# A hybrid decoder layer with expert rows: 32 columns move from the small token group to the large one

## The reference, cut to what matters

```
def _trunk(x, ...):
    xn = _rmsnorm(x, g_mix)
    xr, yr, ca, cb, ga, gb = _split_cols(xn @ w_in)
    ... branch_a = (h * gelu(yr)) @ w_a          # RG-LRU branch
    ... branch_b = silu(layernorm(dc)) @ w_b     # convolution branch
    merged = sigmoid(ga) * branch_a + sigmoid(gb) * branch_b
    x = x + merged @ w_out
    x = x + _peer(_rmsnorm(x, g_ffn), w_q, keys1, keys2, u_tab, v_tab)
    return _rmsnorm(x, g_final)

def block(xb):                                   # _peer, 8 heads, 16 experts per head
    q = (xb @ w_q).reshape(128, 8, 2, 128)
    s1 = einsum('thd,hkd->thk', q[:, :, 0], keys1); s2 = ... q[:, :, 1], keys2
    v1, i1 = top_k(s1, 16); v2, i2 = top_k(s2, 16)
    sv, si = top_k(v1[..., :, None] + v2[..., None, :], 16)
    e = i1[si // 16] * 128 + i2[si % 16]; g = softmax(sv)
    act = gelu(einsum('thkd,td->thk', u_tab[e], xb))
    return einsum('thk,thkd->td', g * act, v_tab[e])
```

## Time and profile before

| | us |
|---|---|
| median of 3 runs (lowest, highest) | 3867.29 (3864.64, 3870.36) |
| the profiled execution | 3870.63 |
| its span | 3868.8 |
| first product pair of the large group starts | 917.5 |
| last scores of the large group end | 1857.1 |
| first dot of the loop over r | 1912.4 |
| dot 256 of that loop starts | 2791.5 |

### The profile page before, as it was taken

The page is one execution under the profiler, slowest core; times in us unless marked ns, Lnnn a source line. Parts: engine busy times, 40 slices in busy tenths (PEclk is TensorE's granted clock), DMA queues, the critical chain, the costliest instruction groups (busy, mean ns, idle before and its releaser), DMA issues.

```text
span 3868.8 us, 34526 instructions
## 1 busy us (share of the span) xinstructions
PE 3051.7 (79%) x11870; PEld 1937.8 (50%) x11870; DVE 2591.0 (67%) x3611; ACT 586.0 (15%) x1115; POOL 1394.5 (36%) x876
## 2 busy tenths in 40 slices
PE   6999989987999989888345544544179899999993
PEld 6999989975555545555112212222143334444441
DVE  2788830035777766666688887889985556665658
ACT  4444320010010000111100001222250000000000
POOL 2000000003343333324476667666612234434344
PEclk9999999989999999999676677777599999999996
DMA  4222367759899998889899999999849999999998
GB/s 125 85 84 85 97 188 241 238 191 353 327 383 391 369 380 333 321 339 355 339 410 405 407 401 404 357 383 378 316 182 350 365 408 418 421 421 421 421 422 357
DMA packets 394596, 1244.91 MB, mean 322 GB/s; under 512 B 22785, under 2 KB 268289, under 8 KB 268959
## 3 DMA queue, kind: packets, MB, share of 16 engines
q0 software_dynamic: 120720, 876.60, 56.4%
q1 hardware_dynamic: 258944, 356.03, 26.4%
q10 hardware_dynamic: 14815, 10.87, 0.9%
HBM read 1232.26 MB, written 12.00 MB: 322 GB/s over the span
## 4 chain that ended last, share of the span: by engine, by line
DMA 35%; PE 27%; DVE 20%; issue 10%; POOL 5%; ACT 1%; SPq 1%; DVEq 0%; POOLq 0%; ACTq 0%
DMA region<-in_v_tab_dram,region 26%; PE ps L1588 14%; DVE region L1418 6%; DMA region<-in_u_tab_dram,region 5%; POOL region L607 5%; DVE region L1366 4%; PE ps L1571 3%; PE ps L1573 3%; PE ps L1572 3%; DVE region L1357 1%; DMA region<-in_w_q_dram 1%; DMA region<-scores_kept 1%; DVE region L1315 1%; DVE region L1312 1%; DMA region<-in_w_in_dram 1%
## 5 line engine op out<-in xcount | busy, mean ns | idle before, releaser
L607 POOL DMA_INDIRECT region<-in_u_tab_dram,region x544 | 886.8, 1630 | 1488.5 <-DVE region L1357 578.8
L1588 PE MATMUL ps<-region,region 128*128 128x160 f32 (+1 forms) x5120 | 1208.7, 399 | 67.3 <-DMA region<-in_w_out_dram 20.1
L1588 PEld LDWEIGHTS ps<-region,region 128*128 128x128 f32 x5120 | 852.2, 194 | 415.5 <-issue 43.1
L1418 DVE SCALAR_TENSOR_TENSOR region<-region,region 128x2048 f32<-128x2048 f32 x384 | 869.5, 2287 | 105.0 <-DMA region<-in_u_tab_dram,region 104.3
L1818 PE MATMUL ps<-region,region 128*128 128x512 f32 x2048 | 890.4, 597 | 38.8 <-DMA region<-in_v_tab_dram 38.0
L1366 DVE SCALAR_TENSOR_TENSOR region<-region,region,region 128x2048 f32<-128x2048 f32 x224 | 526.8, 2352 | 560.5 <-DMA region<-in_v_tab_dram,region 548.9
L1818 PEld LDWEIGHTS ps<-region,region 128*128 128x128 f32 x2048 | 389.7, 191 | 538.9 <-issue 483.2
L607 POOL DMA_INDIRECT region<-in_v_tab_dram,region x288 | 469.5, 1630 | 423.8 <-DVE region L1366 338.6
L1766 PE MATMUL ps<-region,region 128*128 128x512 f32 x512 | 355.8, 861 | 330.3 <-DMA region<-in_v_tab_dram,region 305.7
L1766 PEld LDWEIGHTS ps<-region,region 128*128 128x128 f32 x512 | 139.2, 285 | 532.2 <-issue 505.9
L1357 DVE SCALAR_TENSOR_TENSOR region<-region,region 128x2048 f32<-128x2048 f32 x160 | 363.0, 2286 | 17.7 <-DMA region<-in_u_tab_dram,region 17.6
(11 more groups left out here) (227 smaller groups left out, 1681.0 us busy)
## 6 DMA issues: line engine op xcount, KB each, us to landing
region<-in_v_tab_dram SPq DMA_DIRECT2D x128, 1024.0 KB
region<-in_w_in_dram SPq DMA_DIRECT2D x192, 512.0 KB
region<-in_w_out_dram SPq DMA_DIRECT2D x64, 512.0 KB
region<-in_w_q_dram SPq DMA_DIRECT2D x64, 512.0 KB
region<-in_w_a_dram SPq DMA_DIRECT2D x32, 512.0 KB
region<-in_w_b_dram SPq DMA_DIRECT2D x32, 512.0 KB
region<-in_u_tab_dram,region POOLq DMA_INDIRECT x544, 12.0
region<-in_x_prompt_dram SPq DMA_DIRECT2D x7, 1024.0 KB, 16.1
```

The lines of the kernel that those rows point to most:

```text
L607: pool.indirect_dma_start(out=slot, out_offset=None, in_=rows_ap, in_offset=bass.IndirectOffsetOnAxis(ap=idx[:, k:k + 1], axis=0)).then_in ...
L1418: stt(out=u_b[s], in0=u_b[s], scalar=1.0, in1=xn_tile(UNITS_A + u), op0=ALU.mult, op1=ALU.mult, accum_out=dots[u % 2][:, k:k + 1]).then_in ...
L1588: last = mm(outs[n][:, 0:WIDTH[g]], wide[s][:, q, n * P:(n + 1) * P], rhs(k), start=(k == 0), stop=(k == n_k - 1))
```

## The change

The small group becomes 128 columns: the last 96 prompt tokens and the 32 samples. The large group becomes `WB` = 416 columns: 384 and the 32 prompt tokens in front of those 96. These 32 prompt tokens are now the folded tile (units 8 and 9); its rows and scores come with the large group. The tile of units 0 to 7 holds 96 prompt tokens and the samples. `ROWS_W` is 128 instead of 96: DVE adds every value row of units 0 to 7, and PE's diagonal products keep the 32 of the folded tile (`ROWS_P` = 32, one every 7 dots). The count of gathers is the same.

```
-NA, NBT = P + TS, 3 * P
-COLS = (slice(NBT, T), slice(0, NBT))
-WIDTH = (NA, NBT)
-TILES = (slice(0, 2), slice(2, 5))
+NBT = 3 * P
+WB = NBT + TS
+PA = P - TS
+COLS = (slice(WB, T), slice(0, WB))
+WIDTH = (P, WB)
+TILES = (slice(0, 1), slice(1, 5))
...
-ROWS_W = 6 * TOPK
+ROWS_W = HEADS * TOPK
-VALUE_AT = {V_LAG + v * (ROWS_A - V_LAG) // ROWS_W: v for v in range(ROWS_W)}
+VALUE_AT = {V_LAG + v: v for v in range(ROWS_W)}
...
-STEPS_NORM = (118, 121)
+STEPS_1, STEPS_2, STEPS_3 = 14, 80, 96
+STEPS_NORM = (STEPS_3, STEPS_3 + 3)
...
-def steps_branch(m):
-    return 14 + 21 * m // 2, 14 + 21 * (m + 1) // 2
+def steps_branch(i):
+    return STEPS_1 + (STEPS_2 - STEPS_1) * i // PAIRS, STEPS_1 + (STEPS_2 - STEPS_1) * (i + 1) // PAIRS
...
-    return 98 + 2 * min(j, 10), 98 + 2 * min(j + 1, 10)
+    return STEPS_2 + (STEPS_3 - STEPS_2) * j // DC, STEPS_2 + (STEPS_3 - STEPS_2) * (j + 1) // DC
...
-    return 121 + 39 * h // HEADS, 121 + 39 * (h + 1) // HEADS
+    first = STEPS_NORM[1]
+    return first + (ROWS_W - first) * h // HEADS, first + (ROWS_W - first) * (h + 1) // HEADS
...
             for p in range(ROWS_A + 1):
+                if p == ROWS_W:
+                    for q in range(SLOTS_V + 1):
+                        small_value(p - 1 + q)
...
-                if p - 1 in VALUE_AT:
-                    v = VALUE_AT[p - 1]
-                    if v >= SLOTS_V:
-                        pool.wait_ge(v_added, v - SLOTS_V + 1)
-                    value_row(v)
+                if p != ROWS_W:
+                    small_value(p - 1 if p < ROWS_W else p - 1 + SLOTS_V)
...
             for h in range(2, HEADS):
-                fifth_tile(h)
                 expert_steps(*STEPS_Q[h])
...
             for h in range(HEADS):
                 expert_steps(*steps_query(h))
+                fifth_tile(h)
+            route(HEADS)
+            expert_steps(ROWS_W, ROWS_A)
...
                 pe.wait_ge(s_read[j], HEADS * g + h + 1)
-                pe.wait_ge(s4_read[j], (h if g == 0 else HEADS) + 1)
-                for t in range(2 + g):
+                pe.wait_ge(s4_read[j], h * g + 1)
+                for t in range(1 + 3 * g):
```

137 lines of the change are left out of this document (75 added, 62 removed).

## The result

The changed kernel takes 4028.05 us in the median of 4 runs (4024.89 to 4029.80), the kernel before 3865.97 (4 runs) on the same chip: a ratio of 1.0419, with a 95% interval of 1.0400 to 1.0437. It is slower by 162 us, where 118 was forecast. The profiled execution has a span of 4026.6 us against 3868.8.

The account below looks back on a forecast made before the run. PE was taken to bound both column groups, DVE and DMA the work up to dot 256. Small group -66, large group +73, gap +180 and loop -69 gave +118 on 3867.3, so 3985 us, range 3925 to 4035.

Parts of the forecast that it names:

- the forecast's own band: Whole kernel: a time of 3960 to 4010 us around the forecast of 3985, chance 0.45.
- rival (2): Large group: handshakes between DVE, ACT and PE slow heads and trips, giving 4010 to 4025 us; chance 0.16.
- Small group, -66: Small group: narrower passes, less norm work and fewer waits start the large group 66 us earlier, at about 851.
- Rival (3): Small group does not shrink, because of PE's weight loads or the full queue: +52 at most, 4037 us; chance 0.07.
- Gap, +180: Last scores to the loop's first dot: late expert steps make it 235 us instead of 55; bounds +135 and +215.
- Rival (1): Gap: gathers keep up and steps run at the queue's rate, 5.2 us a pair, giving 3940 us; chance 0.24.
- Loop over r, -69: Loop over r: 32 fewer value rows save 43 us in the first half and 26 in the second.
- Large group, +73: Large group: wider passes +69, norm work +8, fewer waits for weights -4; last scores at 1864.
- The norm: Large group's norm: work that left the small group comes here, on the path, +8 us.
- takes some of PE's waits for weights; -4: Large group's trips: slightly lower DMA load shortens PE's waits for weights by 4 us; bounds 0 and -20.
- The rest, 0: From dot 256 on: no change; the last stage stays 1077 us.
- Rival (4): Up to dot 256: queues alone decide, making the kernel faster at 3841 us, if DVE's late work is below 900; chance 0.08.

Follow-up runs that it names:

- e2: Changed kernel with POOL issuing each value row's gather one place later among the u gathers (one step ahead, not two): 4004.0 us, ratio 1.0365.
- e5: Kernel before with the folded tile's 32 value rows, their gathers and PE's products for them left out: 3807.8 us, ratio 0.9852.
- e3: Changed kernel's columns (128 and 416) with the kernel before's steps and order; folded tile takes the small group's rows and scores: 3853.7 us, ratio 0.9979.
- e4: Kernel before's columns (160 and 384) with the changed kernel's steps, value-row places and ACT and POOL order: 4039.1 us, ratio 1.0466.
- e11: Changed kernel with value gathers one step ahead, norm's steps from 100, and w_out's steps all before its last six blocks: 3988.5 us, ratio 1.0339.
- e7: Changed kernel with the norm's steps at 100 to 102 and value gathers one step ahead instead of two: 3994.4 us, ratio 1.0328.
- e10: Changed kernel with 10.5 steps instead of 8.25 in each branch trip, ten beside w_out, 108 to 110 in the norm: 4035.8 us, ratio 1.0445.

## Why the prediction was right, and where its sum was short

The forecast for the sign, and the mechanism, hold: PE has no work while DVE does the 32 steps behind the last scores. The range (3925 to 4035) holds the 4028, but the forecast's own band (3960 to 4010) does not: the time fell into the 4010 to 4035 that was kept for rival (2), whose mechanism did not make it. That the range held is partly luck. The time is 43 us above the forecast, and the sum shows where: the small group is 6 us under it, the large group 34 over, the gap 1 under, the loop 17 over.

**Small group, -66.** Measured -72.4. The pass fell to 112 ns (forecast 108.6) and the weights kept up, at 289 GB/s. Rival (3), that the group does not shrink, fell with it. The Trainium skill (TensorE: Matmul & The Clock Gate, "Back-to-back issue gap") says that the weight load and the product set the spacing together, with more than the columns alone would make at 128. These float32 passes don't bear out what I drew from it, that few columns win little: from 160 to 128 columns the spacing fell from 136 to 112 ns, 18% for 20% fewer columns.

**Gap, +180.** Measured +179.3, and its parts agree: the last head's steps 18.4 us after the last scores (25 forecast, 6.6 too much), `fifth_tile` and route 11.3 (12), the cold gather 6.9 (7), steps 128 to 159 with two routes 191.3 (122 + 48 + 14 = 184), the loop's first gather 6.6 (7). Steps with a value row took 7.2 us each (twelve of them from 1973.52 to 2059.8), 6.8 forecast. My own sum for such a step gave 7, and I took 6.8. Rival (1), the queue's rate of 5.2 us a step, fell for this kernel; with the gathers in the order of e2 the same steps took 5.4 to 6.4. Beside it stood my estimate from the Trainium skill (DMA: Bandwidth & Descriptors, "Anatomy of one DMA — SWDGE (gpsimd) path") of 4.4 us for a gather; here again the cold one took 1927.87 - 1921.76 = 6.1 us from issue to use.

**Loop over r, -69.** Measured -52.2 (-29.1 and -23.1 for -43 and -26). The step at fault is the first half: I let it fall to the queue's floor, 379, and added 6. Both e5 and the kernel after stop at 399, with the DMA engines at 0.96 and DVE busy 358. DVE waits 35.8 us for u rows in this half, in 40 waits (61.1 in the kernel before), which with its 358 us of work is nearly the whole 399. I had these waits at 24 (385 less 361). Why the rows still come late with 32 gathers fewer was not taken apart.

**Large group, +73.** Measured +107: this is the term that was mis-sized. By its parts:

| | forecast | measured |
|---|---|---|
| trips | +41.6 - 4 | +45.2 |
| w_out | +13.9 | +18.9 |
| norm | +8 | +32.5 |
| heads | +13.9 | +10.4 |

The widths are right: 64 passes take 22.51 us, 22.5 forecast. *The norm* is where it went wrong: 24 of the 34 us. I priced the folded tile's own work and did not follow the steps that now stand ahead of the last row additions, nor what DVE's steps ask of ACT. The runs divide it: 11.3 us by the columns (e3), 19.6 by the steps (e4), together 31 of 32.5; and e11 takes 22 off the norm of e7 by moving nothing but the place of the steps. The traces divide it alike. The last row addition ends 9.4 us behind PE's way back (0.6 before): 8.8. From it to the first transpose 38.7 us pass (24.6 before), with the 15.1 on the gelu behind ACT's stores: 14.1. The transposes take 17.2 (7.8 before): 9.4. *The trips* have the wrong sign in one term: "takes some of PE's waits for weights; -4". PE's waits for weights went from 28.5 us to 42.8, and its idle time in the trips in all from 32 to 38. e4 shows it apart from the columns: +31 us of trips with the old widths, 21 of them idle time of PE. The gathers come in bursts there, behind DVE's waits for ACT's copy, which my working didn't follow. What of the loss is these bursts and what the order of the gathers was not separated; e10, without the bursts and with more gathers, is slower still in the trips.

**The rest, 0.** Measured -3.4, and as much between other kernels of the same code there (1069 to 1079).

**Rival (2)**, handshakes, named 4010 to 4025, which is nearly what came, but by its own steps it is wrong: it put the loss at PE's waits for `fifth_tile` in the heads, and the heads took 203.2 us, 3.5 less than widths alone would make them; in the trips, where it had the rest, no wait of PE for DVE is left to be seen. The mechanism is real all the same: e3, with more steps to a head, has 29 us of it. A loss from DVE's order did come, at the norm and at 5.0 us of PE's waits for `add_rows` in `w_out`. **Rival (4)**, faster because the queues decide, fell: from the last scores to dot 255 it is 1061 us. But my argument against it was weaker than it looked: DVE is busy 910 of them (156, 358 and 396 in the windows), just above the 900 that I named as the bound, and not 968. The other 151 us DVE stood idle, 79 of them in the gap, most of it waiting for u rows.

**What I said would prove it wrong** did in part: PE does wait for DVE in the large group, for the rows of the norm and 5 us in `w_out`. Steps 128 to 145 in 5 us, and a loop shorter by all of 83 us or by nothing, did not come.

Of the runs with all of the computation none is measurably faster than the kernel before. The best with the new columns and late steps are 3.3 and 3.4% slower (e7 and e11), and the kernel with the columns alone, which gives the folded tile the small group's scores, shows that only 0.2% was to be had even at no price for the late rows.

## What to carry to other kernels

Widening one group of columns and narrowing another only shifted the bound engine's time here (-72 us and, by the widths, +69); ask what moves behind the last product that could cover it, and price that work at the rate that its slots and their order allow (7.2 us a step here, 5.2 by the queue). When work is spread ahead of another engine's inputs, follow the last piece of it to the stage's border: a step in front of the last row addition delays the whole next stage, and what is won there by moving it forward can come back one stage earlier. A mean DMA share hides bursts; look at windows shorter than a trip, and where the queues fall, ask what the engine that frees the slots is waiting for.
